# Projection loop of a hybrid decoder trunk turned by three tiles, with a new tile order and a reworked x stage

## What is computed

```python
u = rmsnorm(h, norm_mix)
z = u @ w_in                      # r, k, v (1024 each), w/a/g features (64+64+160); fox q, k, v (1024 each), f (16)
z_rw = z_rw + (z_prev - z_rw) * mu_shift
y_rw = rwkv7_mixer(z_rw, ...)     # decays, normalised kk, a gated recurrence over time, bonus, group norm
y_fox = fox_mixer(fq, fk, fv, ff + b_f, q_norm, k_norm)   # causal softmax attention with forgetting
h = h + concat(y_rw, y_fox) @ w_out
```

## Time and profile before

| | us |
|---|---|
| median of 3 runs | 2836.48 |
| lowest, highest | 2836.39, 2837.19 |
| the profiled execution | 2838.68 |
| span of its instructions | 2837.0 |
| TensorE busy (x17826 matmuls) | 2745.4 (97%) |
| VectorE busy | 1244.4 (44%) |
| ScalarE busy | 882.0 (31%) |
| GpSimd busy | 165.9 (6%) |

### The profile page before, as it was taken

One profiled execution on the slowest core, in us unless ns is written; L12 is line 12 of the kernel. 1 busy time (PEld: TensorE's weight loads), 2 busy tenths in 40 slices (PEclk: granted clock), 3 DMA queues, 4 the chain that ended last, 5 costly groups with the idle time before them and its releaser, 6 DMA issues.

```text
span 2837.0 us, 46091 instructions
## 1 busy us (share of the span) xinstructions
PE 2745.4 (97%) x17826; PEld 2190.1 (77%) x17826; DVE 1244.4 (44%) x1635; ACT 882.0 (31%) x1300; POOL 165.9 (6%) x172
## 2 busy tenths in 40 slices
PE   8999999999779899999999999999999999999997
PEld 5867777777458867888888888888888888888886
DVE  4365555665524454544322343223432243334444
ACT  4244444444334432422211222112221122223233
POOL 0000000000023200200000000000000000011110
PEclk9999999999879999999999999999999999999998
DMA  6444555454352233333333333333333333333333
GB/s 183 125 132 141 149 149 145 119 148 130 95 167 93 82 104 89 96 97 96 96 96 96 96 96 96 96 96 96 96 96 96 97 97 97 96 97 105 99 93 91
DMA packets 533117, 309.64 MB, mean 109 GB/s; under 512 B 56365, under 2 KB 508613, under 8 KB 532045
## 3 DMA queue, kind: packets, MB, share of 16 engines
q1 hardware_dynamic: 484093, 275.83, 33.8%
q10 hardware_dynamic: 43552, 14.71, 1.9%
q0 software_dynamic: 5424, 18.45, 1.7%
HBM read 272.64 MB, written 36.31 MB: 109 GB/s over the span
## 4 chain that ended last, share of the span: by engine, by line
issue 56%; PE 36%; DVE 2%; POOL 2%; DMA 2%; ACT 1%; SPq 0%; DVEq 0%; POOLq 0%; ACTq 0%
PE acc L563 6%; PE acc L565 6%; PE acc L564 6%; PE acc L913 2%; PE acc L914 2%; PE acc L915 2%; POOL sumsq L1867 2%; PE bank L647 1%; PE bank L634 1%; PE bank L717 1%; PE bank L727 1%; PE bank L662 1%; PE acc L727 1%; DMA w_raw<-in_w_in 1%; PE bank L640 1%
## 5 line engine op out<-in xcount | busy, mean ns | idle before, releaser
L1405 DVE TENSOR_TENSOR w_lo<-w_raw,w_hi 128x1024 fp32r<-128x1024 f32 (+1 forms) x422 | 522.5, 1238 | 1172.3 <-ACT w_hi L1041 1170.8
L1041 ACT ACTIVATE w_hi<-w_raw 128x1024 fp32r<-128x1024 f32 x420 | 444.8, 1059 | 1225.4 <-PE acc L565 1161.2
L563 PE MATMUL acc<-a_hi,w_hi 128*128 128x512 f32 x1824 | 719.5, 394 | 4.4 <-DVE w_lo L1405 4.3
L565 PE MATMUL acc<-a_hi,w_lo 128*128 128x512 f32 x1824 | 711.6, 390 | 0.0
L564 PE MATMUL acc<-a_lo,w_hi 128*128 128x512 f32 x1824 | 711.4, 390 | 0.0
L563 PE MATMUL acc<-b_hi,w_hi 128*128 128x512 f32 x1280 | 498.5, 389 | 0.0
L565 PE MATMUL acc<-b_hi,w_lo 128*128 128x512 f32 x1280 | 498.0, 389 | 0.0
L564 PE MATMUL acc<-b_lo,w_hi 128*128 128x512 f32 x1280 | 498.0, 389 | 0.0
L563 PEld LDWEIGHTS acc<-a_hi,w_hi 128*128 128x128 f32 x1824 | 343.3, 188 | 89.9 <-issue 18.7
L565 PEld LDWEIGHTS acc<-a_hi,w_lo 128*128 128x128 f32 x1824 | 343.2, 188 | 71.8
L564 PEld LDWEIGHTS acc<-a_lo,w_hi 128*128 128x128 f32 x1824 | 343.3, 188 | 71.1 <-issue 1.7
(11 more groups left out here) (267 smaller groups left out, 2151.2 us busy)
## 6 DMA issues: line engine op xcount, KB each, us to landing
w_raw<-in_w_ff SPq DMA_DIRECT2D x256, 512.0 KB, 4.0
w_raw<-in_w_in SPq DMA_DIRECT2D x100, 512.0 KB, 3.8
w_raw<-in_w_out SPq DMA_DIRECT2D x32, 512.0 KB, 3.9
w_raw<-in_w_ple_gate SPq DMA_DIRECT2D x32, 512.0 KB, 3.9
z_d<-ev POOLq DMA_DIRECT2D x50, 256.0 KB, 3.4
ab_d<-ab ACTq DMA_DIRECT2D x8, 1024.0 KB, 7.0
x_c<-ab_d SPq DMA_DIRECT2D x8, 1024.0 KB, 4.9
x_t<-ab_d SPq DMA_DIRECT2D x9, 512.0 KB, 3.9
```

The lines of the kernel that those rows point to most:

```text
L563: mm(dst, wh, hi[:, kt, :], start=kt == 0, stop=False)
L565: last = mm(dst, wl, hi[:, kt, :], start=False, stop=kt == KT - 1)
L1041: A(w_hi[:, s, :, :], w_raw[:, s, :, :], ACT.Copy).then_inc(sg("w_hi_ready"), 1)
L1405: V.tensor_tensor(w_lo[:, s, :, 0:width], w_raw[:, s, :, 0:width], w_hi[:, s, :, 0:width].bitcast(F32), ALU.subtract).then_inc(sg("w_split ...
```

## The change

- **Loop turned.** With `Z_LEAD` = 3 the first three tiles of pair 0 come ahead of the loop (beside `once`, whose steps move from 7..12 to 2..6), the body takes tiles 3, 4, 5 of pair i and 0, 1, 2 of pair i+1, and the last three tiles of pair 7 come behind it with `last_side`. The steps that are left (second logits, both transposes of probabilities, values, bonus) follow after tile 49 in an order of their own; probabilities, maxima and sums are held for both heads, and two results go to accumulator banks.
- **Tile order** is k, fox q, fox k, fox v, r, v. `load_pair` loads the first three, waits for `ev_free0` at 64 and `ev_free1` at 48, and stands after the first tile's weight units of the body. Fox v, r and v have a load each, after the units of the body's third, fourth and fifth tile, each behind the store that it needs.
- **Side work.** On VectorE receptance moves from 2 to 6, the features `ab` are all made at 7, values at 8. The factor -exp(-0.5) goes into the scale of ScalarE's exps, which write over `cum` and `lw`. ScalarE issues the store of `ab` at 7, of values and bonus at 9, after `normalize`. TensorE's `weigh_values(i, 0)` moves from 8 to 9.
- **x stage.** The 48 narrow columns have their own buffers `nw`, and their matmuls run slice by slice, four slices behind the transposes. Squares are summed four slices at a time, each into 32 rows of a bank; ScalarE copies the bank and one matmul with ones adds and spreads it. SyncE loads the first tile's units after slices 6 and 8. GpSimd stores `h` in four parts as they become ready.

The core of the diff, in the order of the file (SyncE, TensorE, ScalarE, VectorE, GpSimd):

```diff
-Z_COLUMNS = (DR, 0, 2 * DR, N_SHIFT, N_SHIFT + DR, N_SHIFT + 2 * DR)
+Z_COLUMNS = (DR, N_SHIFT, N_SHIFT + DR, N_SHIFT + 2 * DR, 0, 2 * DR)
+Z_LEAD = 3
+DECAY = float(np.exp(-0.5))
...
+                if f == 3:
+                    for cols, n0, n in ((slice(0, 32), N_SHIFT - 32, 32), (slice(32, 48), N_SHIFT + 3 * DR, 16)):
+                        sp.dma_start(nw[:, :, cols], w_in_v[:, :, n0:n0 + n]).then_inc(sg("narrow_landed"), 16)
+                if f in (6, 8):
+                    first_unit(f // 2 - 3)
...
-                sp.wait_ge(sg("ev_free0"), i * 48 + 80)
-                sp.sem_inc(sg("sp_waits_taken"), 1)
-                sp.wait_ge(sg("ev_free1"), i * 48 + 64)
-                sp.sem_inc(sg("sp_waits_taken"), 1)
+                sp.wait_ge(sg("ev_free0"), i * 48 + 64)
+                sp.sem_inc(sg("waits_taken"), 1)
+                sp.wait_ge(sg("ev_free1"), i * 48 + 48)
+                sp.sem_inc(sg("waits_taken"), 1)
                 sp.wait_ge(sg("side_inputs_used"), i + 1)
-                for t, dst in enumerate((kin, rin, vin, qin, k_in)):
-                    dst = dst[:, 1:] if t < 3 else dst[:, :]
-                    sp.dma_start(dst, z_d[bass.ds(i * Z_PAIR + (2 + t), 1), :, :].rearrange("a p t -> (a p) t")).then_inc(sg("side_landed"), 16)
...
+            def load_receptance(i):
+
+                sp.wait_ge(sg("ev_free0"), i * 48 + 80)
+                load_tile(i, 4, rin[:, 1:], "rin_landed")
...
-            for t in range(2, Z_PAIR):
-                pair_units(0, 2 + t, t)
+            pair_units(0, 4, 2)
             with sp.Fori(0, NPAIR - 1) as i:
                 for t in range(Z_PAIR):
-                    pair_units(i, 2 + Z_PAIR + t, t)
+                    pair_units(i, 2 + Z_LEAD + t, (Z_LEAD + t) % Z_PAIR)
                     if t == 0:
                         load_pair(i)
-                    if t == 1:
+                    if t == 2:
                         load_fox_v(i)
-
-            for s in range(2):
-                unit(s, w_out_v[:, UK:, s * P:(s + 1) * P], Z_ODD + 2 * M_OUT + s)
-            load_pair(NPAIR - 1)
+                    if t == 3:
+                        load_receptance(i)
+                    if t == 4:
+                        load_value(i)
+
+            for t in range(Z_LEAD):
+                pair_units(NPAIR - 1, 2 + Z_LEAD + t, Z_LEAD + t)
+                if t == 0:
+                    load_pair(NPAIR - 1)
             load_fox_v(NPAIR - 1)
-
-
...
-            def sum_squares(f):
-
-                pe.wait_ge(sg("squares_ready"), f + 1)
-                mm(bank[3][:, :], ones, sq[:, f % 2, :], start=f == 0, stop=f == KT - 1).then_inc(sg("x_squares_summed"), 1)
+            def sum_squares(g):
+
+                pe.wait_ge(sg("squares_ready"), NB * g + NB)
+                for j in range(NB):
+                    last = mm(bank[3][32 * j:32 * j + 32, :], const(C_ONE, 32), squares[j], start=g == 0, stop=g == H_X - 1)
+                last.then_inc(sg("x_squares_summed"), 1)
+
+            def narrow(k):
+
+                if k == 0:
+                    pe.wait_ge(sg("narrow_split"), 1)
+                pe.wait_ge(sg("operand_split"), k + 1)
+                mm(bank[0][0:48, :], nw_hi[:, k, :], a_hi[:, k, :], start=k == 0, stop=False)
+                mm(bank[0][0:48, :], nw_hi[:, k, :], a_lo[:, k, :], start=False, stop=False)
+                return mm(bank[0][0:48, :], nw_lo[:, k, :], a_hi[:, k, :], start=False, stop=k == KT - 1)
 
             for f in range(KT):
                 b = f % 4
...
-            pair_tiles(0, 2, once)
+                    store_fox(i)
+
+            def last_side(i, at):
+
+                if at == 1:
+                    square_qk(i)
+                if at == 2:
+                    gate_decays(i)
+                    head_roots(i)
+                if at == 3:
+                    high_rows(i)
+                    decays(i)
+                if at == 5:
+                    take_values(i)
+                    exps(i, 0)
+
+            pair_tiles(0, 2, once, Z_LEAD)
             with act.Fori(0, NPAIR - 1) as i:
-                pair_tiles(i, 2 + Z_PAIR, side)
...
+            for f in range(KT):
+                act.wait_ge(sg("h_ready"), f + 1)
+                A(a_hi[:, f, :], h[:, f, :], ACT.Copy, scale=pc("norm_mix", f)).then_inc(sg("operand_hi_ready"), 1)
+                if f >= NB:
+                    act.wait_ge(sg("x_squares_summed"), f // NB)
+                A(squares[f % NB], h[:, f, :], ACT.Square).then_inc(sg("squares_ready"), 1)
+                if f == 2:
+                    act.wait_ge(sg("narrow_landed"), 32)
+                    A(nw_hi[:, :, :], nw[:, :, :], ACT.Copy).then_inc(sg("narrow_hi_ready"), 1)
+                if f == 9:
+                    hi_unit(0, 0, 0)
+            hi_unit(1, 0, 0)
+            act.wait_ge(sg("x_squares_summed"), H_X)
+            A(sumsq[:, :], bank[3][:, :], ACT.Copy).then_inc(sg("x_sums_taken"), 1)
             root(0)
...
                 if at == 7:
+                    store_features(i)
                     take_probs(i, 0)
                 if at == 8:
-                    act.wait_ge(sg("features_made"), i + 1)
-                    act.dma_start(ab_d[:, :, :, bass.ds(i, 1), :].rearrange("p c k a t -> p (c k) (a t)"), ab[:, :, :, :].rearrange("p c k t -> p (c k) t")).then_inc(sg("features_stored"), 16)
-                    act.dma_start(v_d[:, :, bass.ds(i, 1), :].rearrange("c p a t -> p c (a t)"), vs[:, :].rearrange("p (c t) -> p c t", c=NC)).then_inc(sg("features_stored"), 16)
-                    act.dma_start(bonus_d[bass.ds(i, 1), :, :].rearrange("a p t -> (a p) t"), bon[:, :]).then_inc(sg("features_stored"), 16)
                     exps(i, 1)
                 if at == 9:
                     normalize(i, 1)
+                    store_values(i)
                 if at == 10:
                     take_probs(i, 1)
                 if at == 12:
-                    act.wait_ge(sg("heads_done"), i * 2 + 2)
-                    act.wait_ge(sg("fox_stored"), i * 16 + 16)
-                    A(og[:, :], bank[1][:, :], ACT.Copy).then_inc(sg("fox_taken"), 1)
-                    act.wait_ge(sg("fox_taken"), i + 2)
...
+                pair_tiles(i, 2 + Z_LEAD, side)
+            i = NPAIR - 1
+            pair_tiles(i, 2 + Z_LEAD, last_side, Z_LEAD)
+            normalize(i, 0)
+            take_probs(i, 0, last_prob_banks)
+            exps(i, 1)
+            normalize(i, 1)
+            store_features(i)
+            take_probs(i, 1, last_prob_banks)
+            store_values(i)
+            store_fox(i)
 
...
+            def receptance(i):
+
+                dve.wait_ge(sg("rin_landed"), i * 16 + 16)
+                then(shift(rs[:, :], rin, pc("mu", i)))
+                V.scalar_tensor_tensor(t2[:, :], rs[:, :], pc("r_k", i), km[:, :], ALU.mult, ALU.mult).then_inc(sg("rk_ready"), 1)
...
+            def features(i):
+
+                dve.wait_ge(sg("ab_stored"), i * 16 + 16)
+                dve.wait_ge(sg("exps_ready"), i * 3 + 3)
+                V.tensor_tensor(ab[:, :, 1, :], by_chunk(rs), by_chunk(e_in), ALU.mult)
+                dve.wait_ge(sg("qk_ready"), i * 3 + 1)
+                V.scalar_tensor_tensor(ab[:, :, 0, :], by_chunk(kk), -1.0, by_chunk(lw), ALU.mult, ALU.mult)
+                then(V.tensor_tensor(dif[:, :], kk[:, :], av[:, :], ALU.mult))
+                V.tensor_tensor(ab[:, :, 2, :], by_chunk(dif), by_chunk(cum), ALU.mult)
+                then(V.tensor_tensor(ab[:, :, 3, :], by_chunk(km), by_chunk(cum), ALU.mult))
+                dve.sem_inc(sg("features_made"), 1)
+
+            def values(i, summed=bank[1]):
+
+                dve.wait_ge(sg("vin_landed"), i * 16 + 16)
+                dve.wait_ge(sg("features_stored"), i * 32 + 32)
+                then(shift(vs[:, :], vin, pc("mu", i + 16)))
+                dve.wait_ge(sg("bonus_summed"), i + 1)
+                V.scalar_tensor_tensor(bon[:, :], summed[:, :], float(HD), vs[:, :], ALU.mult, ALU.mult).then_inc(sg("bonus_taken"), 1)
 
             def side(i, at):
 
...
+            i = NPAIR - 1
+            pair_tiles(i, 2 + Z_LEAD, last_side, Z_LEAD)
+            invert_sums(i, 0)
+            softmax(i, 1)
+            receptance(i)
+            features(i)
+            invert_sums(i, 1)
+            values(i, acc[1])
...
-            pool.wait_ge(sg("h_ready"), KT)
             for k in range(4):
+                pool.wait_ge(sg("h_ready"), 4 * k + 4)
```

More of the change, by code:

```diff
@@ L318, in build @@
     NB = 4
+    H_X = KT // NB
     squares = [sq[:, 0, :], sq[:, 1, :], ev[:, 0, :], ev[:, 1, :]]
@@ new lines, in spread_rows, with first_logits @@
+            def spread_rows(i):
+                pe.wait_ge(sg("row_split"), i + 1)
+                for n in range(3):
+                    mm(bank[2 + n][:, :], spread_r[:, n, :], row_hi[0:6, :], start=True, stop=False)
+                    last = mm(bank[2 + n][:, :], spread_r[:, n, :], row_lo[0:6, :], start=False, stop=True)
```

(33 more changed lines are left out.)

405 lines of the change are left out of this document (232 added, 173 removed).

## The result

The changed kernel takes **2916.82 us** (median of 4 runs, 2915.65 to 2918.24) beside 2836.43 for the kernel before on the same chip: a ratio of **1.0284**, 95% interval 1.0266 to 1.0302. It is 80 us slower; 2932 was forecast, with a range of 2903 to 2957. The profiled execution took 2915.65 us, its span 2914.0, against 2837.0 before.

What follows compares the result with a forecast made beforehand. TensorE was taken as the bound, with projection tiles back to back. 2838.7 - 12 (x stage) + 114 (stalls) + 14 (small steps) - 20.5 (last pair) = 2934.2, against the median 2932 us; range 2903 to 2957.

Steps and rivals of the forecast that it cites:

- The deciding cost: Loop: SyncE waits for tile m-1 with weight units queued behind; 15.0 us lost a pair, 8 times, 114 net.
- Store to first load: Loop: from a tile's store on POOL's queue to SyncE's first side load, 4.18 us.
- Issues ahead of the first unit: Loop, SyncE: from first side load to the next weight unit, 4.06 us for seven issues.
- First load to next tile: Loop: side loads, weight parts, key squares and head sums until tile m+1 starts, 21.8 us.
- the bound of 16.5: Loop: upper bound of the stall a pair, in us, if TensorE stays slow into the tile after idling longer.
- x stage: Before the first full tile: it starts at 41 us against 51.45, with the slow start a gain of 12 us.
- the low end of 5: x stage: gain of some 5 us if square sums do not overlap, or changing tiling mode drains TensorE.
- Small steps: Loop: waiting bonus matmul 0.9 us, low weights late by 1.8; taken as 2 us a turn, 14 in all.
- Last pair: Tail: state stage begins 29.5 us after the last tile instead of 58.3; less 8.3 of side work, 20.5 gained.
- The late loads: Rival, loop: late loads cost nothing, the eight stalls vanish, 2812 us; turning point 3.0 us a pair; chance 7%.
- The second rival: Loop: only side inputs are late, weight units not held behind `load_pair`; 8 us a pair, 2876 us; chance 5%.
- cascade: Rival, loop: late units push fox, receptance and value loads; second stall of 4 us a pair, 2964 us; chance 4%.

Runs made afterwards that it cites:

- direct_keys: Changed kernel, with VectorE writing the pair's third tile also straight into the side work's buffer, so `load_pair` waits only for tiles up to m-2: 2813.38 us.
- before_nearer: Kernel before the change, with `load_pair` inside the loop waiting for one more stored tile (m-1 instead of m-2): 2934.22 us, ratio 1.0349.
- narrow_queue: Changed kernel, with the two narrow weight loads of the x stage issued by GpSimd at the start instead of by SyncE: 2918.06 us.
- keys_bonus: Kernel of direct_keys, with the bonus matmuls half a tile later on TensorE, behind the transposes of the probabilities: 2803.03 us, ratio 0.9887.
- keys_features: Kernel of direct_keys, with the last pair's receptance and features ahead of its second softmax on VectorE: 2811.31 us.
- all_four: Changed kernel with direct third tile, later bonus matmuls, GpSimd narrow loads with later narrow product, and last pair's features before its second softmax: 2803.07 us, ratio 0.9891.
- units_first: Changed kernel, with loads needing no tile, then tile m+1's weight units, issued before SyncE's wait; only three tile loads behind it: 2847.37 us, ratio 1.0038.

## Why the prediction was right

**The deciding cost was named and placed rightly**: the wait is one tile nearer, the units stand behind it, the key squares behind those. direct_keys removes it alone and before_nearer adds it alone, and the loss goes and comes with it. The stall was forecast 1.9 us too long: 13.1 on average where 15.0 stood, and this is 15.3 of the 18.8 us by which the sum is too high. The rest is the last pair's 3.6; the 3.2 that the x stage lacks and the 3.1 that the small steps have too many cancel, by luck.

- **Store to first load**, 4.18 in the prediction by the earlier trace rows: 2.79 here. This term was mis-sized. The row of before was taken while weight units were in flight, and after the change there are none. By the fit in the Trainium skill, "DMA: Bandwidth & Descriptors", Anatomy of one DMA, such a store takes 2.6, an estimate; the prediction let the row decide, and the page was the nearer.
- **Issues ahead of the first unit**, 4.06: 4.21. **First load to next tile**, 21.8: 21.2.
- **The clock** falls to the 1.2 GHz level before the head sums, as forecast. They take 4.1 us, not 5.2, since the clock comes back while they run; it is full when the next tile starts, and the bound of 16.5 was not needed.

**x stage, -12 forecast, -8.8 found.** The failed step is "the last low operand ... comes at 37.5": it comes at 40.5 (the last two start at 39.14). VectorE was taken to lose 2.2 us by its two splits and little by waits. In the trace it waits for transposes three times, 1.60, 2.46 and 2.15 us: TensorE itself first waits for x 3.07 us, then for the split of the narrow weights 2.55 us, and its first slices run at half pace. The x loads take 4.6 us from issue to landing (median), where the kernel before has 2.8; the forecast gave this 1.5 us in all. narrow_queue shows that the queue hold, found in this trace, is not the limit by itself. How the missing 3 us divide among these stays open. The overlap of the square sums was taken rightly: four take 0.99 us, and one alone took 0.96 in the kernel before, so neither the low end of 5 nor the page's drain came about.

**Small steps, +14 forecast, +10.9 found.** The wait of the bonus matmuls was right (0.9 against 0.98, and 1.2 with what surrounds it; keys_bonus gets most of it back). The failed step is the 1.8 us by which the stores of values and bonus were to make the low weights late: they cost nothing. The store of values, 4.21 us long in the earlier trace rows, takes 0.39 in the loop (781.04). In the kernel before it is issued 0.6 to 0.8 us behind the 1 MB store of features, and all eight take 4.0 to 4.2; here it is issued 15.7 us behind it. That the 1 MB store is the reason was not tested apart.

**Last pair, -20.5 forecast, -24.1 found.** The steps run as written, 3.6 us faster: the features are stored at +15.4 after the last tile, not +18: the issue stands behind `normalize` in ScalarE's order, but goes out at 867.06 while the activations of `normalize` still run until 869. The stores of values and bonus, 4 us behind that of the features, take 1.7 us, not 5.2. The end is set, as forecast, by the features' way through DRAM (store at 867.06, `x_t` loaded at 873.67), with the last weighing 0.9 us ahead of it; keys_features and all_four show that nothing is gained by bringing the features forward.

**Rivals.** The late loads were not hidden: a stall of 13 us is far above the turning point of 3.0. What that rival forecast for a kernel without stalls, 2812, is near what direct_keys measured, 2813.4; the other terms of the sum hold together, with errors of about 3 us each that partly cancel. The second rival's setting, weights not held, was built only nearly, as units_first: 4.3 us a pair, below its 8, with two broadcast rows and the lora weights taken out of the wait too. No cascade appeared.

## What to carry to other kernels

When a loop is turned, count for each queue which tile a wait needs at its new place, and list what stands behind it: here one count, a tile nearer, held the next weights back and cost 105 us, more than twice what all of the change's good parts gave. Before a value goes through DRAM and back to the same core, ask whether the engine that makes it can write it where it is used: one extra write of 0.7 us beside a tile replaced a way of 13 us. Price a transfer from a row in which the queues are as full as they will be after the change.

## What the runs showed of the hardware

- **A store and the load that waits for it** take 2.79 and 2.66 us from issue to issue where the DMA engines are a quarter busy (share 0.24 in the changed kernel, 0.25 in before_nearer, the same within 0.1 in all turns of their loops), and 3.5 to 4.4 where weight units are in flight (0.72 in the turn shown of units_first, 0.62 in that of the kernel before). No run changes the share alone.

```profile
703.30:706.10 2.80, 2.80 (x14) 2.33 (x13) 0.00 (x0) 0.00 (x0) 0.54 (x1) 1.00 0.24 94
```
```profile
647.00:651.20 4.20, 4.20 (x22) 3.47 (x20) 0.08 (x1) 2.49 (x5) 0.54 (x1) 1.00 0.62 187
```

- **Two loads of 48 narrow columns** hold the issuing queue for 5.12 us on SyncE, behind four x loads that take 2.06 together, and 2.47 us (1.54 to 4.0, in narrow_queue) when GpSimd issues them beside the same x loads.
- **Square sums of 32 columns** overlap four by four. Each is a float32 product of two matmuls; the first matmuls of all four start within 0.02 us (27.19 and 27.20), the second ones within 0.02 again (27.64 and 27.65), and the next operation follows at 28.18. So four take 0.99 us, where one full product of 128 columns takes 0.96 in the kernel before, from 30.93 to 31.89. The Trainium skill, "TensorEngine Tiling (Array Packing)", Key Properties, says that a change of tiling mode drains TensorE; here nothing of it is visible above 0.1 us: the 0.03 more, and a first step of 0.28 instead of 0.23 behind the group.

```profile
27.20 0.62 PE L622 MATMUL bank<-ev,cst 128*32 128x512 f32 x2
27.64 0.60 PE L622 MATMUL bank<-sq,cst 128*32 128x512 f32 x2
27.65 0.60 PE L622 MATMUL bank<-ev,cst 128*32 128x512 f32 x2
28.18 0.44 PE L630 MATMUL bank<-a_hi,nw_hi 128*48 128x512 f32 x1
```
```profile
31.89 0.38 PE L606 MATMUL bank<-cst,prow 128*128 128x128 f32 x2
```
